# Softmax probabilities left unscaled, their transposes done as fp32 products with a diagonal matrix of reciprocal row sums

## The reference

```python
s = jnp.einsum('bqhd,bkhd->bhqk', qf[:, q0:kend], kf[:, :kend]) * scale
bias = c[:, :, q0:kend, None] - c[:, :, None, :kend]
mask = (q0 + jnp.arange(Q_BLOCK))[:, None] >= jnp.arange(kend)[None, :]
s = jnp.where(mask, s + bias, -jnp.inf)
p = jax.nn.softmax(s, axis=-1)
outs.append(jnp.einsum('bhqk,bkhd->bqhd', p.astype(v.dtype), v[:, :kend]))
```

## Time and profile before

| what | value |
|---|---|
| median of three executions | 1069.19 us |
| the profiled execution: its own time | 1067.87 us |
| the profiled execution: span, first to last instruction | 1066.1 us |
| mean granted TensorE clock | 0.999 |
| busy: PE, PEld, DVE, ACT, POOL | 99%, 88%, 72%, 52%, 4% of the span |
| attention slots | about 415 to 542 us of the span |

### The profile page before, as it was taken

The page is one execution under the profiler, slowest core; times in us unless marked ns, Lnnn a source line. Parts: engine busy times, 40 slices in busy tenths (PEclk is TensorE's granted clock), DMA queues, the critical chain, the costliest instruction groups (busy, mean ns, idle before and its releaser), DMA issues.

```text
span 1066.1 us, 16095 instructions
## 1 busy us (share of the span) xinstructions
PE 1052.3 (99%) x6441; PEld 941.2 (88%) x6441; DVE 771.8 (72%) x929; ACT 549.9 (52%) x797; POOL 45.2 (4%) x98
## 2 busy tenths in 40 slices
PE   9999999999999999999999999999999999999997
PEld 7899999998888988888878888889899999988886
DVE  6988989979986573566654323458778878779964
ACT  7455455456644683577683222344444554556642
POOL 2000000000001210000000000011000000000001
PEclk9999999999999999999999999999999999999999
DMA  9523323450151554232115344315524224450051
GB/s 303 191 79 113 125 80 102 168 198 7 57 183 41 179 151 106 73 87 61 40 43 155 99 118 158 99 40 178 159 80 144 94 80 134 144 198 0 21 178 79
DMA packets 118215, 121.21 MB, mean 114 GB/s; under 512 B 6624, under 2 KB 98800, under 8 KB 118144
## 3 DMA queue, kind: packets, MB, share of 16 engines
q1 hardware_dynamic: 114928, 115.47, 34.6%
q10 hardware_dynamic: 2240, 2.11, 0.8%
q0 software_dynamic: 976, 2.66, 0.7%
HBM read 111.80 MB, written 6.29 MB: 111 GB/s over the span
## 4 chain that ended last, share of the span: by engine, by line
PE 86%; DVE 5%; ACT 3%; issue 2%; DMA 2%; SPq 1%; POOL 1%; ACTq 0%; DVEq 0%; POOLq 0%
PE bank L1777 11%; PE bank L1779 11%; PE bank L1778 11%; PE bank L1691 9%; PE bank L1681 7%; PE bank L1683 6%; PE bank L1682 6%; PE bank L1839 5%; PE bank L1840 5%; PE bank L1841 5%; PE bank L1931 1%; PE bank L1930 1%; PE bank L1929 1%; PE bank L1746 1%; PE bank L1748 1%
## 5 line engine op out<-in xcount | busy, mean ns | idle before, releaser
L1777 PE MATMUL bank<-tc,w_hi 128*128 128x256 f32 x576 | 163.0, 283 | 0.0
L1778 PE MATMUL bank<-tc,w_hi 128*128 128x256 f32 x576 | 163.0, 283 | 0.0
L1779 PE MATMUL bank<-tc,w_lo 128*128 128x256 f32 x576 | 163.0, 283 | 0.0
L1101 DVE TENSOR_TENSOR w_lo<-raw,w_hi 128x1024 fp32r<-128x1024 f32 x69 | 84.2, 1221 | 90.6 <-ACT w_hi L638 90.5
L1777 PE MATMUL bank<-u_hi,w_hi 128*128 128x256 f32 x432 | 122.5, 283 | 2.8 <-DVE scr L1295 2.8
L1779 PE MATMUL bank<-u_hi,w_lo 128*128 128x256 f32 x432 | 122.3, 283 | 0.0
L1778 PE MATMUL bank<-u_lo,w_hi 128*128 128x256 f32 x432 | 122.2, 283 | 0.0
L1681 PE MATMUL bank<-u_hi,w_hi 128*128 128x512 f32 x296 | 117.5, 397 | 0.4 <-issue 0.2
L1683 PE MATMUL bank<-u_hi,w_lo 128*128 128x512 f32 x296 | 115.6, 390 | 0.0
L1682 PE MATMUL bank<-u_lo,w_hi 128*128 128x512 f32 x296 | 115.4, 390 | 0.0
L1777 PEld LDWEIGHTS bank<-tc,w_hi 128*128 128x128 f32 x576 | 110.6, 192 | 0.0
(11 more groups left out here) (291 smaller groups left out, 2313.6 us busy)
## 6 DMA issues: line engine op xcount, KB each, us to landing
raw<-in_w_in SPq DMA_DIRECT2D x40, 512.0 KB, 3.9
raw<-in_ffn_w_down SPq DMA_DIRECT2D x20, 512.0 KB, 6.3
h<-in_ffn_w_gate SPq DMA_DIRECT2D x9, 1024.0 KB, 5.3
h<-in_ffn_w_up SPq DMA_DIRECT2D x9, 1024.0 KB, 8.9
raw<-in_ffn_w_gate SPq DMA_DIRECT2D x9, 1024.0 KB, 5.5
raw<-in_ffn_w_up SPq DMA_DIRECT2D x9, 1024.0 KB, 8.2
h<-in_ffn_w_down SPq DMA_DIRECT2D x8, 512.0 KB, 6.3
og_place<-in_ffn_w_down SPq DMA_DIRECT2D x8, 512.0 KB, 6.5
```

Source lines behind the costliest of these rows:

```text
L1101: V.tensor_tensor(w_lo[:, slot(u), :], raw[:, slot(u), :], w_hi[:, slot(u), :].bitcast(F32), ALU.subtract).then_inc(lo_ready, 1)
L1777: mm(dst, w_hi[:, slot(u), w], moving(n, 0, k), start=first and k == 0, stop=False, skip_group_check=True)
L1778: mm(dst, w_hi[:, slot(u), w], moving(n, 1, k), start=False, stop=False, skip_group_check=True)
L1779: last = mm(dst, w_lo[:, slot(u), w], moving(n, 0, k), start=False, stop=k == KD // 2 - 1, skip_group_check=True)
```

## The change

ACT's scaling of the probabilities goes. DVE builds, behind the reciprocal of each step, a diagonal matrix: the fp32 identity with each row multiplied by that row's reciprocal, in one of three buffers (`inv_diag`, 128 x 384 fp32 in all). It signals `probs_ready` in the place of ACT. PE's transposes become ordinary fp32 matmuls of each block of unscaled probabilities with that diagonal matrix, so that the result is transposed and scaled at once.

```diff
+        inv_diag = sb("inv_diag", [P, 3, P])
...
-                if sl < NS:
-                    act.wait_ge(rinv_ready, sl + 1)
-                    nc.scalar.activation(probs[qb], probs[qb], ACT.Copy,
-                                         scale=rinv[:, sl:sl + 1]).then_inc(probs_ready, 1)
...
                     V.reciprocal(rinv[:, sl:sl + 1], rowsum[:, sl:sl + 1]).then_inc(rinv_ready, 1)
+                    if sl >= 3:
+                        dve.wait_ge(pt_ready, sl - 2)
+                    dve.wait_ge(rinv_ready, sl + 1)
+                    V.tensor_scalar(inv_diag[:, sl % 3, :], ident[:, :], rinv[:, sl:sl + 1], None, ALU.mult).then_inc(probs_ready, 1)
...
-                        last = nc.tensor.transpose(bank[:, B_PT[s % 2], n * P:(n + 1) * P],
-                                                   probs[qb][:, kb * P:(kb + 1) * P], ident[:, :])
+                        last = mm(bank[:, B_PT[s % 2], n * P:(n + 1) * P],
+                                  probs[qb][:, kb * P:(kb + 1) * P], inv_diag[:, s % 3, :], start=True, stop=True)
```

## The result

The changed kernel takes 1074.88 us (median of five, 1074.49 to 1077.81); the kernel before, in five executions beside it, 1069.63 us (1067.85 to 1071.11). The ratio is 1.0055, 95% interval 1.0042 to 1.0067: slower by 4.5 to 7.2 us. Forecast were 1076.0 us and 1071.5 to 1081.5. The profiled executions take 1074.49 and 1067.87 us, 6.6 us apart, where the sum had +7.1.

The account below looks back on a forecast made before the run. The prediction took PE's closed stream to bound the attention: +9.0 us for products less 1.9 us of waits gave +7.1 us, 1076.3 us on the median shown, given as 1076.0 us, range 1071.5 to 1081.5 us.

Parts of the forecast that it names:

- the sum: Whole kernel: +9.0 us of products on PE less 1.9 us of waits, +7.1 us.
- PE's stream as the bound: Attention: PE's stream is closed except at two waits; ACT and DVE set at most 2.33 us of it.
- The price of the product: 80 blocks on PE: an fp32 product costs 0.22 us against 0.11 for a transpose, +9.0 us in all.
- The end of GLA's group: After GLA's fp32 products: about 0.09 us for the step to 64 rows, left out because 128 rows follow here.
- What comes back of the waits: PE's two waits in 446 to 492 us shrink by 1.6 to 2.33 us; 1.9 us taken.
- the first wait: PE's matmul at 484.92 us, read as starting 1.69 us late behind ACT's copies for GLA.
- PE's own delay of 3.4 us: In 446 to 492 us PE gets 30 of the 80 blocks, 30 x 0.112 = 3.4 us later.
- ACT's relief: Dropping L1043's 17.9 us of ACT scaling is nearly worthless; at most 1.3 us on the chain, within the 2.33 us.
- A cheap second half: Rival for PE's products: a product costs 0.16 us, +2.1 us in all, 1071.3 us; chance 8%.
- four transposes for a product: Rival for PE's products: a product costs four transposes, 0.44 us, +24 us in all, 1093 us; chance 3%.
- DVE as the bound: Rival in the attention's slots: the diagonal matrix makes PE wait, 6.9 us on top of 9.0, 1085.1 us; chance 8%.
- The rival on the faster side: Attention: products cost what transposes cost, ACT's relief removes the waits, 1066.9 us; needs a product under 0.14 us; chance 4%.

Follow-up runs that it names:

- Products twice: The changed kernel with each product of a block issued twice in a row into the same place; 1094.83 us, ratio 1.0252 to the kernel before.
- the fp32r product: The changed kernel with probabilities and diagonal matrix stored as fp32r, one matmul for a block; 1067.89 us, ratio 0.9984 to the kernel before.
- The unused matrix: The kernel before with the diagonal matrix built by DVE behind each reciprocal but used by nobody; 1070.86 us, ratio 1.0010.
- products with the identity, ACT scales: The kernel before with its transposes replaced by fp32 products with the plain identity, ACT's scaling kept; 1075.51 us, ratio 1.0056.
- fp32r, matrix on GpSimd: The kernel with fp32r probabilities and matrix, the matrix built by GpSimd in place of DVE; 1067.04 us, ratio 0.9984 to the kernel before.

## Why the prediction was right

**PE's stream as the bound.** Right. The whole difference lies between the first scores and the last product with the values, and the run without any scaling shows what the other side is worth: 1.9 us.

**The price of the product.** Right: 0.22 us for a block, from two matmuls at 0.111. The end of GLA's group, 0.09 us more, was rightly left out: it belongs to the change from 128 to 64 rows, which this group has not. Products twice and the fp32r product show from both sides that each matmul costs 0.11 us and that nothing else adds to it. Stage: 80 x 0.112 = 9.0 us, less 2.2 us, is 6.7 with unrounded terms; measured 6.8.

**What comes back of the waits.** The mechanism was right, the size a little under. The waits themselves were read 0.09 us too long: the start of L1998 was set against a pace of 0.23 us, and 0.32 us is what that place takes with nothing waited for. So the first wait was 1.60 us and not 1.69, the sum 2.24 us and not 2.33. All 2.24 us came back where 1.9 was taken, a value between 1.6 and 2.33. The 1.6 rested on charging DVE's 11 x 0.286 = 3.1 us in full to its loop with ACT. The unused matrix shows that this costs PE's waits only 0.46 us. That is the term that was mis-sized. PE's own delay of 3.4 us was also a little high for the first wait, since 27 of the 30 blocks stand ahead of it, 3.0 us; it was enough.

**ACT's relief.** Right that it is nearly worthless beside the products: with ACT's scaling kept, the time is the same. Alone it is worth 1.9 us of stage, out of the same 2.24 us, and can't be won twice. That is more than the bound of 1.3 us taken from the three pieces of L1043 on the chain: the first wait gave back 1.40 us, and the second 0.52 us beside it.

**The rivals.** A cheap second half, four transposes for a product, and DVE as the bound are each refuted: by the pace of 0.111 us, by the same, and by the closed stream of PE after. The rival on the faster side named its point of decision rightly, 0.14 us for a product: the fp32r product, at 0.115 us, lies below it, and that kernel's stage is 0.8 us shorter than before. The rule of the Trainium skill (the page "TensorE: Matmul & The Clock Gate", section "Terms") that transpose mode makes fp32 four times as fast does not show here: for whole blocks of 128 x 128 the ratio from start to start is two, 0.22 to 0.11 us.

**What the forecast could not see.** By the medians the change costs 5.25 us, 1.9 under the sum; by the profiled executions 6.6. The interval of 4.5 to 7.2 us holds both. The granted clock of the single executions accounts for most of the difference. A stretch of 3.4 us at half clock (last section) takes 1.7 us and lowers an execution's mean granted clock by 0.0016; an execution with a mean of 0.999 or more has no such stretch in full. The profiled execution from which the sum was taken had none, but of 44 executions of the kernel before, beside the experiments, only 13 are at 0.999 or more; of the changed kernel's five, four are. The forecast put 1.3 us between profiled execution and median on both sides of the change, and after it they lie 0.4 us apart. Compared at 0.999 or more alone, the times follow the stages:

| run | executions at 0.999 or more | median of these, less that of before | stage, less that of before |
|---|---|---|---|
| scaling left out | 3 of 7 | -2.1 us | -1.9 us |
| products with the identity, ACT scales | 4 of 5 | +7.0 us | +7.0 us |
| fp32r probabilities and matrix | 7 of 11 | -1.0 us | -0.8 us |
| each product twice | 1 of 4 | +25.2 us | +24.6 us |
| ACT's scaling on GpSimd | 9 of 11 | -1.4 us | -1.3 us |
| fp32r, matrix on GpSimd | 10 of 11 | -1.2 us | -1.4 us |

The unused matrix, which lengthens the waits, has 1 of 11. So the medians of the kernels with shorter waits at GLA seem to hold, beside the shorter stage, fewer stretches of low clock. That the shorter waits are the reason fits these counts, but "each product twice", with waits closed and 1 of 4, does not fit, and no run tests it alone.

## What to carry to other kernels

Before folding a multiplication into a transpose on TensorE, count the matmuls and weight loads that the type needs: an fp32 product was two of each at 0.11 us, an fp32 transpose one, and where TensorE's stream is closed that difference counts in full, while the engine that is relieved gives back no more than TensorE had waited for it. Read that sum of waits first, from start to start in the timeline: but for the clock it is the most that any relief of the others can win, and two edits can't both win it. If it is worth having, move the work to an engine that is idle (here GpSimd: 1.3 us of stage, 2.0 us by the medians), rather than onto the one that is full.

## What the runs showed of the hardware

In some executions the granted clock fell to its lower level, 1.2 GHz, for 3.4 us, and each time PE had waited before. In the kernel with the unused matrix PE had waited 2.0 us (2.35 us from start to start, less 0.32) until 485.56 us and again 0.67 us until 492.45, and windows of all engines (the third number from the end is the granted clock) show the fall some 10 us behind the first of these:

```profile
488.00:492.00 4.00, 3.94 (x23) 3.13 (x21) 3.71 (x11) 2.46 (x5) 0.00 (x0) 1.00 0.29 66
492.00:496.00 4.00, 3.55 (x26) 3.39 (x27) 3.02 (x7) 1.80 (x5) 0.00 (x0) 0.91 0.00 0
496.00:499.00 3.00, 3.00 (x11) 2.47 (x10) 2.46 (x6) 2.88 (x7) 0.00 (x0) 0.55 0.69 172
```

```profile
496.93 0.63 PE L1685 MATMUL bank<-u_lo,w_hi 128*128 128x512 f32 x1
497.36 0.63 PE L1686 MATMUL bank<-u_hi,w_lo 128*128 128x512 f32 x1
```

A mean of 0.91 over 4 us and of 0.55 over 3 us is 0.7 + 2.7 = 3.4 us at half clock. Matmuls of 512 columns started every 0.43 us there in place of 0.23, so such a stretch costs 3.4 / 2 = 1.7 us where PE's stream is closed. Four more of the nine profiled executions had one, each 1.4 us or less behind the end of PE's wait at the start of the second network's down projection, a wait for DVE that no edit here touches. In the run without scaling:

```profile
945.00 0.28 PE L1775 MATMUL bank<-tc,w_lo 128*128 128x256 f32 x1
947.44 0.39 PE L1773 MATMUL bank<-u_hi,w_hi 128*128 128x256 f32 x1 [2.16 <-DVE scr L1291]
```

From start to start the wait at this place was 2.02 us (each product twice), 2.19 (fp32r), 2.22 (scaling on GpSimd) and 2.44 (no scaling) where the clock fell, and 1.68 (the changed kernel), 1.83 (before), 2.12 (products with the identity), 2.19 (fp32r with the matrix on GpSimd) and 2.36 (the unused matrix) where it stayed at its upper level:

```profile
948.56 0.28 PE L1782 MATMUL bank<-tc,w_lo 128*128 128x256 f32 x1
950.92 0.39 PE L1780 MATMUL bank<-u_hi,w_hi 128*128 128x256 f32 x1 [2.08 <-DVE scr L1296]
```

So the length of the wait alone does not decide it; what does is open. (Every profile also ends at the lower level, for the last 0.2 to 3.8 us of its span, the changed kernel's for 2.0 us.) A wait on PE can cost more than its own length, and single executions of one kernel differ by 1.7 us for a reason that need not lie in the edit.
